# Latent projections of a fused transformer kernel: loads in order of use and in pieces, the first two weight units side by side, one PSUM bank per output

## The chip, the cores and the metric

The kernel runs on one core of a Trainium2 chip. The metric is the device time of one execution in microseconds. The time before is the median of three executions.

## The reference, cut to what matters

The reference is a stack of three transformer blocks on 512 tokens of width 1024. The first one begins with latent attention. Its opening, which the change touches, is:

```python
h = rms_norm(x, attn_pre_g[0])
a = h @ w_a                                   # 1024 x (384 + 256 + 64)
cq, ckv, kr = jnp.split(a, [384, 640], axis=-1)
q  = rms_norm(cq, g_q) @ w_uq                 # 8 heads of 128 + 64
kv = rms_norm(ckv, g_kv) @ w_ukv              # 8 heads of 128 + 128
# rotary embedding of the 64-wide parts with cos, sin of positions; attention; w_o;
# y = x + rms_norm(attention @ w_o); FFN (silu(gate) * up) @ down; a second attention block
# with a relative bias, and its FFN; a third block: gated attention, a 31-tap convolution,
# and an FFN with a 3-tap convolution on gate and up; a last rms_norm
```

## The kernel before, in words

Activations lie transposed: 128 rows of the width on the partitions, 512 tokens along the free axis, so x is eight tiles of 128x512. All products are of fp32 accuracy made from three products of shorter floats: every operand is split into a high and a low part, and `product` issues high x high, low x high, high x low (lines 350 to 352).

The weights come as a stream of 307 units of 128x1024 (eight 128x128 blocks each), in the order in which TensorE uses them. Each unit passes four engines, through two buffers of each kind:

- SP loads it into `raw` (`load_units`, line 321); the load of unit u waits for the low part of unit u-2.
- ACT rounds it into `whi` in `round_unit` (line 326). Each call takes the next unit, `turn["act"]`, and waits for its load and for TensorE's last product of unit u-2. The calls stand at fixed places in ACT's program, between its other work.
- POOL subtracts and writes the low part `wlo` (`low_units`, line 336).
- TensorE waits for `wlo` in `next_unit` (line 342) and does the unit's 24 matmuls.

ACT's program before calls `round_unit` 8 times in `latents_act`, then 12 times in the MLA heads, 8 in its output projection, 66 in the first FFN, 24 in block B, 8 in its output projection, 66 in the second FFN, 28 in the first half of block C, 7 in its heads, 16 in the merge and 66 in the last FFN: 309 calls. Calls beyond unit 306 do nothing. TensorE uses 6, 12, 8, 66, 24, 8, 66, 28, 7, 16 and 66 units in the same stages.

Between the blocks stand the joins j0 to j3 (`join_pe`, `join_act`, `join_dve`): the residual is added tile by tile, each new tile of x is split and multiplied by one unit at once, its square is summed on TensorE (`pe_sum`, line 463), and at the end `act_root` and `dve_inverse` make the norm's factor. `join_act` has no call of `round_unit`. After j0 and j2 ACT's next work is `ffn_act`, whose first statement is a call; after j1 it is `b_first_act`, after j3 `c_first_act`, with a call first as well.

In the latents, TensorE (`latents_pe`, line 523) multiplies unit 0 by the tiles of x as these are split, with a sum of squares after each tile, then units 1 to 5 (cq, cq, ckv, ckv and the rotary key), with a sum for each earlier output in between. The outputs take banks 0, 1 and 2 in turn. DVE (`latents_dve`) makes the low parts of x and, between them, steps of the sine and cosine tables (`dve_table`). ACT (`latents_act`) issues five loads, rounds unit 0, splits and squares the tiles of x, and makes the sines.

In the last FFN (`ffn_act`, `ffn_dve` with `conv`) each step has a gate unit and an up unit. DVE scales a half (L458), ACT applies Identity with a gain (L984), DVE adds two taps (L1016, L1019), ACT applies Silu (L991), DVE multiplies (L1027) and splits (L1029, L1031). ACT's order in a step is: call, Identity of the gate, call, Identity of up, Silu.

Of the kernel before, what the change touches and what calls it, by code (L numbers as in the profile page):

```python
# [125 lines left out]
def column_map(items):  # L126
    at, where = 0, {}
    for name, n in items:
# [5 lines left out]
GAINS = [("pre0", 8), ("post0", 8), ("fpre0", 8), ("fpost0", 8), ("gq", 3), ("gkv", 2), ("kvsrc", 8),  # L134
# [4 lines left out]
CONSTS = [("ident", P), ("ones", P), ("cdist", 4 * 32), ("cmask", 4 * 32), ("cvalid", 4 * 32), ("inv", 1),  # L139
          ("sgn", 1), ("eps", 1), ("dist", T), ("maskA", T)]  # L140
# [68 lines left out]
def build(nc, x_in, pos_in, stream, gains_in, consts_in, rel_in, w1_in, out):  # L209
# [83 lines left out]
    def gg(name, k=0, n=1):  # L293
        return gn[:, GAIN_AT[name][0] + k:GAIN_AT[name][0] + k + n]

    ident, ones = cc("ident"), cc("ones")


    raw_in = [Signal(nc, f"raw_loaded{j}", 16) for j in range(2)]
    x_got = [Signal(nc, f"x_loaded{j}", 16) for j in range(2)]  # L300
    gains_got, consts_got = Signal(nc, "gains_loaded", 16), Signal(nc, "consts_loaded", 16)
# [12 lines left out]
    every = raw_in + x_got + bias_got + w1_got + [  # L314
        gains_got, consts_got, pos_got, mask_got, rel_got, rel_put, bias_put, out_put, w_hi, w_lo, proj, summed, scored,
# [174 lines left out]
    ang, kk_, rr = rope_tmp  # L490

    def dve_table(e, n):

        if n:
            e.wait_ge(*(made.at("sin") if n == 9 else made.at("cos") if n == 16 else formed.at(("table", n - 1))))
# [11 lines left out]
        elif n in (5, 12):  # L507
            op = e.scalar_tensor_tensor(rr[:, :], kk_[:, :], -c1, ang[:, :], ALU.mult, ALU.add)
        elif n in (6, 13):
            op = e.scalar_tensor_tensor(rr[:, :], kk_[:, :], -c2, rr[:, :], ALU.mult, ALU.add)  # L510
        elif n in (7, 14):
            op = e.scalar_tensor_tensor(rr[:, :], kk_[:, :], -c3, rr[:, :], ALU.mult, ALU.add)
        elif n == 8:
            op = e.tensor_scalar(rr[:, :], rr[:, :], PI32, -PI32, ALU.min, ALU.max)
        elif n == 15:
            e.tensor_scalar(rr[:, :], rr[:, :], float(np.pi / 2), None, ALU.add).then_inc(*formed.done("quarter"))
            e.wait_ge(*formed.at("quarter"))
            op = e.tensor_scalar(rr[:, :], rr[:, :], PI32, -PI32, ALU.min, ALU.max)
# [3 lines left out]

    def latents_pe(e):
        u = next_unit(e)
        for k in range(KD):
            e.wait_ge(*low.at(("pre0", k)))
            mm = product(e, u, k, bank[0][:, :], hh[:, k, :], hl[:, k, :], k == 0, k == KD - 1)
            if k == KD - 1:
                mm.then_inc(*proj.done(("a", 0), ("unit", u)))
            e.wait_ge(*squared.at(("x", k)))  # L530
            pe_sum(e, 7, tmp[k % 2][:, :], k == 0, k == KD - 1, ("x", k))
        for m in range(1, 5):
            if m >= 3:
                e.wait_ge(*evicted.at(("a", m - 3)))
            project(e, m % 3, hh, hl, ("a", m))
            e.wait_ge(*squared.at(("a", m - 1)))
            if m == 4:
                e.wait_ge(*stats.at((("x", 7), "mean")))
            pe_sum(e, 6 if m < 4 else 7, tmp[(m - 1) % 2][:, :], m in (1, 4), m == 3, ("a", m - 1))
        e.wait_ge(*evicted.at(("a", 3)))  # L540
        project(e, 0, hh, hl, "kr")
        e.wait_ge(*squared.at(("a", 4)))
        pe_sum(e, 7, tmp[0][:, :], False, True, ("a", 4))

    def latents_act(e):
        e.dma_start(gn[:, :], gains_in).then_inc(*gains_got.done(0))
        e.dma_start(cst[:, :], consts_in[:, 0:n_fixed]).then_inc(*consts_got.done(0))
# [1273 lines left out]
```

## Time and profile before

| | before |
|---|---|
| time, median of 3 runs | 2263.82 us (2262.23 to 2268.28) |
| profiled execution, its own time | 2264.33 us |
| its span | 2262.3 us |
| TensorE (PE) busy | 2137.6 us, 94% |
| DVE busy | 1031.2 us, 46% |
| ACT busy | 750.2 us, 33% |
| POOL busy | 750.2 us, 33% |
| DMA | 178.59 MB, mean 79 GB/s |

The span is what the trace covers; the time of that same execution is 2.0 us more. Busy times are sums over the whole span and hide which engine is waited for at which place. A row of a timeline gives start, duration, engine, line of the kernel, instruction, output and inputs, and in brackets how long the engine had been idle and whom it had waited for.

### The profile page before, as it was taken

How to read it: one execution, taken by the hardware profiler on the slowest of the kernel's cores; microseconds unless marked ns; L12 is line 12 of the kernel's file. 1: busy time of each engine (PE TensorE's matmuls, PEld its weight loads, DVE VectorE, ACT ScalarE, POOL GpSimd, SP SyncE). 2: the span in 40 equal slices, each digit the busy share in tenths (PEclk: the TensorE clock that was granted, in tenths of full speed). 3: DMA queues.
4: the chain of work that ended last, by engine and by line, in shares of the span. 5: the costliest groups of instructions: out<-in, count | busy, mean ns of one | idle time of the engine just before them, and what ended most of it. 6: DMA issues, size and time to landing. Idle time of an engine off the chain costs nothing.

```text
span 2262.3 us, 22596 instructions
## 1 busy us (share of the span) xinstructions
PE 2137.6 (94%) x8948; PEld 1620.6 (72%) x8948; DVE 1031.2 (46%) x1620; ACT 750.2 (33%) x1213; POOL 750.2 (33%) x311
## 2 busy tenths in 40 slices
PE   6898999999989999999999998898899999999998
PEld 4554778888856776668888885676655587888886
DVE  5543254442134333254444006994544356777511
ACT  4443332222234333332222223122554434333321
POOL 2211334444422222224444442432110143444442
PEclk9998999999999999999999999897799999999999
DMA  3410223232211222113232232221100122233232
GB/s 128 133 54 29 74 67 102 93 102 95 94 64 64 71 75 75 52 57 101 93 101 95 94 102 84 75 75 36 39 29 19 37 94 84 94 97 99 93 102 84
DMA packets 51815, 178.59 MB, mean 79 GB/s; under 512 B 5472, under 2 KB 5488, under 8 KB 51456
## 3 DMA queue, kind: packets, MB, share of 16 engines
q1 hardware_dynamic: 45264, 163.07, 22.2%
q10 hardware_dynamic: 6448, 14.09, 1.8%
q8 instruction: 71, 1.16, 0.2%
q14 instruction: 32, 0.26, 0.0%
HBM read 175.00 MB, written 6.33 MB: 80 GB/s over the span
## 4 chain that ended last, share of the span: by engine, by line
PE 81%; DVE 14%; ACT 3%; issue 1%; DMA 0%; POOL 0%; DVEq 0%; SPq 0%; ACTq 0%
PE bank L350 22%; PE bank L352 22%; PE bank L351 22%; PE bank L373 6%; DVE tmp L1352 4%; PE bank L438 4%; PE bank L424 2%; PE bank L464 1%; DVE hl L481 1%; DVE x L926 1%; DVE tmp L1656 1%; DVE tmp L924 1%; PE bank L832 1%; DVE rs L477 1%; ACT swapA L625 1%
## 5 line engine op out<-in xcount | busy, mean ns | idle before, releaser
L339 POOL TENSOR_TENSOR wlo<-raw,whi 128x1024 fp32r<-128x1024 f32 x307 | 750.0, 2443 | 1490.5 <-ACT whi L334 1490.4
L350 PE MATMUL bank<-hh,whi 128*128 128x512 f32 x1576 | 639.5, 406 | 58.2 <-DVE hl L481 29.4
L334 ACT ACTIVATE whi<-raw 128x1024 fp32r<-128x1024 f32 x307 | 324.9, 1059 | 1076.7 <-PE bank L352 1070.8
L351 PE MATMUL bank<-hl,whi 128*128 128x512 f32 x1576 | 622.7, 395 | 0.0
L352 PE MATMUL bank<-hh,wlo 128*128 128x512 f32 x1576 | 621.6, 394 | 0.0
L350 PEld LDWEIGHTS bank<-hh,whi 128*128 128x128 f32 x1576 | 301.6, 191 | 158.6 <-issue 50.5
L351 PEld LDWEIGHTS bank<-hl,whi 128*128 128x128 f32 x1576 | 302.1, 192 | 65.1 <-issue 5.1
L352 PEld LDWEIGHTS bank<-hh,wlo 128*128 128x128 f32 x1576 | 301.5, 191 | 64.7
L458 DVE TENSOR_TENSOR tmp<-bank,rs 128x512 f32<-128x512 f32 x159 | 109.3, 689 | 229.4 <-PE bank L352 224.9
L350 PE MATMUL bank<-fh,whi 128*128 128x512 f32 x528 | 205.4, 389 | 0.0
L351 PE MATMUL bank<-fl,whi 128*128 128x512 f32 x528 | 205.4, 389 | 0.0
L352 PE MATMUL bank<-fh,wlo 128*128 128x512 f32 x528 | 205.4, 389 | 0.0
L1027 DVE TENSOR_TENSOR tmp<-tmp,tmp 128x512 f32<-128x512 f32 x66 | 121.4, 1839 | 48.6 <-ACT tmp L991 46.3
L351 PEld LDWEIGHTS bank<-fl,whi 128*128 128x128 f32 x528 | 99.1, 188 | 20.7
L352 PEld LDWEIGHTS bank<-fh,wlo 128*128 128x128 f32 x528 | 99.1, 188 | 20.5
L350 PEld LDWEIGHTS bank<-fh,whi 128*128 128x128 f32 x528 | 99.1, 188 | 20.4
L1352 DVE SCALAR_TENSOR_TENSOR tmp<-zpad,gn,tmp 128x512 f32<-128x512 f32 x116 | 110.6, 1023 | 0.0
L1039 DVE COPY y<-bank 128x512 f32<-128x512 f32 x16 | 11.0, 687 | 204.1 <-PE bank L352 204.1
L1016 DVE SCALAR_TENSOR_TENSOR tmp<-tmp,gn,tmp 128x511 f32<-128x511 f32 x44 | 80.5, 1828 | 45.1 <-ACT tmp L984 45.1
L432 ACT ACTIVATE PT<-bank 128x128 f32<-128x128 f32 (+3 forms) x160 | 66.8, 435 | 101.5 <-PE bank L424 99.8
L350 PE MATMUL bank<-oh,whi 128*128 128x512 f32 x192 | 75.7, 394 | 5.1 <-DVE ol L1596 2.2
L352 PE MATMUL bank<-oh,wlo 128*128 128x512 f32 x192 | 75.4, 393 | 0.0
(210 smaller groups left out, 2180.7 us busy)
## 6 DMA issues: line engine op xcount, KB each, us to landing
raw<-stream SPq DMA_DIRECT2D x307, 512.0 KB, 3.4
bias_scratch<-rel_scratch ACTq DMA_DIRECT2D x1, 4096.0 KB, 19.0
biasB<-bias_scratch ACTq DMA_DIRECT2D x16, 256.0 KB, 3.9
x<-x_in SPq DMA_DIRECT2D x2, 1024.0 KB, 9.8
w<-w_in ACTq DMA_DIRECT2D x2, 1024.0 KB, 5.9
out<-y ACTq DMA_DIRECT2D x8, 256.0 KB, 2.2
cst<-consts_in ACTq DMA_DIRECT2D x1, 577.5 KB, 7.1
gn<-gains_in ACTq DMA_DIRECT2D x1, 318.5 KB, 4.3
```

The costliest lines, as they stand in the source:

```text
L334: e.activation(whi[u % 2][:, :], raw[u % 2][:, :], ACT.Copy).then_inc(*w_hi.done(u))
L339: e.tensor_tensor(wlo[u % 2][:, :], raw[u % 2][:, :], whi[u % 2][:, :].bitcast(F32), ALU.subtract)\
L350: e.matmul(o, wh, h, start=first, stop=False)
L351: e.matmul(o, wh, l, start=False, stop=False)
L352: return e.matmul(o, wl, h, start=False, stop=last)
L373: mm = e.matmul(bank[b][:, SPOT[t][1]:SPOT[t][1] + W(t)], qf[:, t * P:(t + 1) * P], kf[:, 0:W(t)], start=i == 0, stop=i == len(pieces) - 1)
L432: e.activation(PT[:, 0:t + 1, t * P:(t + 1) * P], bank[b][:, 0:W(t)].rearrange("p (k c) -> p k c", c=P), ACT.Copy).then_inc(*spread.done(( ...
L438: mm = e.matmul(bank[7][r0:r1, k * P:T], vf(k), PT[:, k, k * P:T], start=first and k == 0, stop=last and k == QT - 1, skip_group_check=not ...
L458: e.tensor_tensor(dst, bank[bk][:, :], r[:, :], ALU.mult).then_inc(*evicted.done(key))
L1016: e.scalar_tensor_tensor(acc[:, 1:T], u[:, 0:T - 1], gg("fdw", (r * KF + j) * 3 + 1), acc[:, 1:T], ALU.mult, ALU.add).then_inc(*formed.don ...
L1027: e.tensor_tensor(u[:, :], u[:, :], g[:, :], ALU.mult).then_inc(*formed.done((key, "product", j)))
L1352: e.scalar_tensor_tensor(s, zp[:, tap:tap + T], gg("dw", c * TAPS + tap), s, ALU.mult, ALU.add)\
```

## The change

- `GAINS` and `CONSTS` are reordered, so that what the latents need comes first, and both are loaded in two pieces; ACT issues seven loads instead of five. SP issues unit 0 first, then x in four pieces of two tiles, with unit 1 behind the second piece.
- Unit 0 is rounded and its low part made in two halves (`w_hi` and `w_lo` get a key 0.5). The second half is rounded behind the first tile of x.
- `latents_pe` runs units 0 and 1 side by side: at step k tile k by unit 0, the sum of tile k-1, tile k-2 by unit 1. Each of the five outputs has a bank of its own (0 to 4), kr takes bank 0 again, the sums use banks 6 and 7. The last sum (of output 4) is moved into `mla_pe`, behind the first MLA unit. That unit no longer waits for the low part of output 4, the second one does.
- The cosine's argument gets a tile of its own, `quarter`. Sine and cosine are made one after the other, behind the root of x. DVE does two table steps after each of the eight tiles.
- The calls of `round_unit` in `latents_act` stand at other places.

```diff
     def low_units(e):
-        for u in range(n_units):
+        e.wait_ge(*w_hi.at(0.5))
+        e.tensor_tensor(wlo[0][:, 0:512], raw[0][:, 0:512], whi[0][:, 0:512].bitcast(F32), ALU.subtract).then_inc(*w_lo.done(0.5))
+        e.wait_ge(*w_hi.at(0))
+        e.tensor_tensor(wlo[0][:, 512:1024], raw[0][:, 512:1024], whi[0][:, 512:1024].bitcast(F32), ALU.subtract)\
+            .then_inc(*w_lo.done(0))
+        for u in range(1, n_units):
...
-    def next_unit(e):
+    def next_unit(e, part=0):
         u = turn["pe"]
         turn["pe"] += 1
-        e.wait_ge(*w_lo.at(u))
+        e.wait_ge(*w_lo.at(part or u))
         return u
...
     def latents_pe(e):
-        u = next_unit(e)
+        u, v = next_unit(e, 0.5), turn["pe"]
+        for k in range(KD + 2):
+            if k == KD // 2:
+                e.wait_ge(*w_lo.at(u))
+            if k == 2:
+                next_unit(e)
+            if k < KD:
+                e.wait_ge(*low.at(("pre0", k)))
+                mm = product(e, u, k, bank[0][:, :], hh[:, k, :], hl[:, k, :], k == 0, k == KD - 1)
+                if k == KD - 1:
+                    mm.then_inc(*proj.done(("a", 0), ("unit", u)))
+            if 1 <= k <= KD:
+                if k == 1:
+                    e.wait_ge(*consts_got[0].at(0))
+                e.wait_ge(*squared.at(("x", k - 1)))
+                pe_sum(e, 7, tmp[(k - 1) % 2][:, :], k == 1, k == KD, ("x", k - 1))
+            if k >= 2:
+                mm = product(e, v, k - 2, bank[1][:, :], hh[:, k - 2, :], hl[:, k - 2, :], k == 2, k == KD + 1)
+        mm.then_inc(*proj.done(("a", 1), ("unit", v)))
+        project(e, 2, hh, hl, ("a", 2))
+        project(e, 3, hh, hl, ("a", 3))
+        for m in range(2):
+            e.wait_ge(*squared.at(("a", m)))
+            pe_sum(e, 6, tmp[m % 2][:, :], m == 0, False, ("a", m))
+        project(e, 4, hh, hl, ("a", 4))
+        e.wait_ge(*squared.at(("a", 2)))
+        pe_sum(e, 6, tmp[0][:, :], False, True, ("a", 2))
+        e.wait_ge(*evicted.at(("a", 0)))
+        project(e, 0, hh, hl, "kr")
+        e.wait_ge(*squared.at(("a", 3)))
+        e.wait_ge(*stats.at((("x", 7), "mean")))
+        pe_sum(e, 7, tmp[1][:, :], True, False, ("a", 3))
...
     def latents_act(e):
-        round_unit(e)
-        e.wait_ge(*gains_got.at(0))
-        e.wait_ge(*consts_got.at(0))
+        e.wait_ge(*raw_in[0].at(0))
+        e.activation(whi[0][:, 0:512], raw[0][:, 0:512], ACT.Copy).then_inc(*w_hi.done(0.5))
+        e.wait_ge(*gains_got[0].at(0))
         for k in range(KD):
-            if k == 4:
-                round_unit(e)
-            if k % 4 == 0:
-                e.wait_ge(*x_got[k // 4].at(0))
+            if k % 2 == 0:
+                e.wait_ge(*x_got[k // 2].at(0))
             e.activation(hh[:, k, :], x[:, k, :], ACT.Copy, scale=gg("pre0", k)).then_inc(*high.done(("pre0", k)))
+            if k == 0:
+                e.activation(whi[0][:, 512:1024], raw[0][:, 512:1024], ACT.Copy).then_inc(*w_hi.done(0))
+                turn["act"] += 1
             if k >= 2:
                 e.wait_ge(*summed.at(("x", k - 2)))
             act_square(e, tmp[k % 2], x[:, k, :], ("x", k))
-            if k == 4:
-                e.wait_ge(*formed.at(("table", 8)))
-                e.activation(sinT[:, :], rr[:, :], ACT.Sin).then_inc(*made.done("sin"))
+            if k == 0:
+                round_unit(e)
         act_root(e, rs[0], ("x", 7))
         round_unit(e)
+        e.wait_ge(*formed.at(("table", 15)))
+        e.activation(sinT[:, :], rr[:, :], ACT.Sin).then_inc(*made.done("sin"))
+        e.activation(cosT[:, :], quarter[:, :], ACT.Sin).then_inc(*made.done("cos"))
+        round_unit(e)
         for m in range(5):
-            if m:
-                round_unit(e)
-            if m == 3:
-                act_root(e, rs[1], ("a", 2))
...
-            if m == 0:
-                e.wait_ge(*formed.at(("table", 15)))
-                e.activation(cosT[:, :], rr[:, :], ACT.Sin).then_inc(*made.done("cos"))
+            if m == 1:
+                round_unit(e)
+            if m == 2:
+                round_unit(e)
+            if m == 3:
+                act_root(e, rs[1], ("a", 2))
         e.wait_ge(*formed.at("rel_ends"))
         e.dma_start(rel_dram, rel[:, :]).then_inc(*rel_put.done(0))
         round_unit(e)
...
     def mla_pe(e):
         mla_unit_pe(e, 0, 0)
+        e.wait_ge(*squared.at(("a", 4)))
+        pe_sum(e, 7, tmp[0][:, :], False, True, ("a", 4))
         mla_unit_pe(e, 1, 0)
...
     def sync_program(e):
         x_v = x_in.rearrange("(k p) t -> p k t", p=P)
-        e.dma_start(x[:, 0:4, :], x_v[:, 0:4, :]).then_inc(*x_got[0].done(0))
         e.dma_start(raw[0][:, :], stream[0, :, :]).then_inc(*raw_in[0].done(0))
-        e.dma_start(x[:, 4:8, :], x_v[:, 4:8, :]).then_inc(*x_got[1].done(0))
-        e.dma_start(raw[1][:, :], stream[1, :, :]).then_inc(*raw_in[1].done(1))
+        for k in range(0, KD, 2):
+            e.dma_start(x[:, k:k + 2, :], x_v[:, k:k + 2, :]).then_inc(*x_got[k // 2].done(0))
+            if k == 2:
+                e.dma_start(raw[1][:, :], stream[1, :, :]).then_inc(*raw_in[1].done(1))
         load_units(e)
```

## Rows read from the trace of the kernel before

**Rows 1.** The page: span, and the group of the low parts (busy, mean ns).

```profile
span 2262.3 us, 22596 instructions
...
L339 POOL TENSOR_TENSOR wlo<-raw,whi 128x1024 fp32r<-128x1024 f32 x307 | 750.0, 2443 | 1490.5 <-ACT whi L334 1490.4
```

**Rows 2.** Timeline of the start, and the first MLA unit (start us, us).

```profile
3.62 1.28 ACT L334 ACT_TABLE_LOAD   x1 [3.62 <-issue]
10.58 1.06 ACT L334 ACTIVATE whi<-raw 128x1024 fp32r<-128x1024 f32 x1 [5.68 <-DMA raw<-stream]
11.72 2.36 POOL L339 TENSOR_TENSOR wlo<-raw,whi 128x1024 fp32r<-128x1024 f32 x1 [11.28 <-ACT whi L334]
...
14.77 0.76 PE L350 MATMUL bank<-hh,whi 128*128 128x512 f32 x1 [14.77 <-DVE hl L481]
...
69.94 0.80 PE L350 MATMUL bank<-cqh,whi 128*128 128x512 f32 x1
```

**Rows 3.** The chain that ended last, in the latents (start us, us).

```profile
16.39 1.71 PE bank L464 x2
...
46.70 0.86 PE bank L464 x2
47.56 0.23 PE bank L350
```

**Rows 4.** Timeline of the end of join j0, DVE, ACT and POOL.

```profile
296.20 0.69 DVE L469 TENSOR_SCALAR rs<-bank 128x512 f32<-128x512 f32 x1 [2.58 <-PE bank L464]
...
296.92 0.63 ACT L473 ACTIVATE rs<-rs 128x512 f32<-128x512 f32 x1 [3.57 <-DVE rs L469]
297.46 1.04 ACT L334 ACTIVATE whi<-raw 128x1024 fp32r<-128x1024 f32 x1
...
298.58 2.40 POOL L339 TENSOR_TENSOR wlo<-raw,whi 128x1024 fp32r<-128x1024 f32 x1 [26.79 <-ACT whi L334]
```

**Rows 5.** A gap of TensorE, and the stretch behind it (PE, PEld, DVE, ACT, POOL, PEclk, DMA).

```profile
61.40 1.92 PE L464 MATMUL bank<-tmp,cst 128*128 128x512 f32 x2 [2.01 <-ACT tmp L461]
...
61.40:65.00 3.60, 3.60 (x7) 2.17 (x8) 2.81 (x3) 2.09 (x3) 2.37 (x1) 0.53 0.00 0
```

**Rows 6.** Timeline of TensorE behind join j1.

```profile
694.30 0.77 PE L350 MATMUL bank<-h2h,whi 128*128 128x512 f32 x1 [4.28 <-DVE h2l L481]
```

**Rows 7.** Timeline of the merge, first tile.

```profile
1798.24 0.69 DVE L1653 TENSOR_TENSOR tmp<-bank,gsig 128x512 f32<-128x512 f32 x1 [7.50 <-PE bank L352]
...
1802.42 0.63 ACT L1636 ACTIVATE hh<-tmp 128x512 fp32r<-128x512 f32 x1 [3.06 <-DVE tmp L1656]
```

**Rows 8.** Timeline of one step of the last FFN, by engine.

```profile
2019.74 0.69 DVE L458 TENSOR_TENSOR tmp<-bank,rs 128x512 f32<-128x512 f32 x1 [0.36 <-PE bank L352]
2021.60 2.29 DVE L1016 SCALAR_TENSOR_TENSOR tmp<-tmp,gn,tmp 128x511 f32<-128x511 f32 x1 [1.17 <-ACT tmp L984]
2023.92 0.75 DVE L1019 SCALAR_TENSOR_TENSOR tmp<-tmp,gn,tmp 128x510 f32<-128x510 f32 x1
2024.78 0.69 DVE L1027 TENSOR_TENSOR tmp<-tmp,tmp 128x512 f32<-128x512 f32 x1
...
2020.77 0.80 ACT L984 ACTIVATE tmp<-tmp,gn 128x512 f32<-128x512 f32 x1
2021.47 0.62 ACT L991 ACTIVATE tmp<-tmp 128x512 f32<-128x512 f32 x1
...
2020.94 2.40 POOL L339 TENSOR_TENSOR wlo<-raw,whi 128x1024 fp32r<-128x1024 f32 x1 [2.90 <-ACT whi L334]
```

**Rows 9.** Timeline of TensorE and POOL in block C, two rows.

```profile
1430.99 0.76 PE L350 MATMUL bank<-hh,whi 128*128 128x512 f32 x1 [3.51 <-POOL wlo L339]
...
1454.91 7.14 POOL L339 TENSOR_TENSOR wlo<-raw,whi 128x1024 fp32r<-128x1024 f32 x1 [6.16 <-ACT whi L334]
```

**Rows 10.** Landing of the pieces of x; the chain's first transfer.

```profile
DMA to landing us min/median/max: 7.3/9.8/12.4
...
1.23 9.33 DMA raw<-stream
```

More of the change, by code:

```diff
@@ L296, in build @@
     ident, ones = cc("ident"), cc("ones")
+    N_FIRST, C_FIRST = GAIN_AT["kvsrc"][0], CONST_AT["cdist"][0]
     raw_in = [Signal(nc, f"raw_loaded{j}", 16) for j in range(2)]
-    x_got = [Signal(nc, f"x_loaded{j}", 16) for j in range(2)]
-    gains_got, consts_got = Signal(nc, "gains_loaded", 16), Signal(nc, "consts_loaded", 16)
+    x_got = [Signal(nc, f"x_loaded{j}", 16) for j in range(4)]
+    gains_got, consts_got = ([Signal(nc, f"{n}_loaded{j}", 16) for j in range(2)] for n in ("gains", "consts"))
     pos_got, mask_got = Signal(nc, "positions_loaded", 16), Signal(nc, "mask_loaded", 16)
@@ L490, in build @@
     ang, kk_, rr = rope_tmp
+    quarter = sb("rope_quarter", [P, T], Y + 4 * KB)
     def dve_table(e, n):
         if n:
-            e.wait_ge(*(made.at("sin") if n == 9 else made.at("cos") if n == 16 else formed.at(("table", n - 1))))
+            e.wait_ge(*(made.at("sin") if n == 16 else formed.at(("table", n - 1))))
         if n == 0:
@@ L507, in dve_table @@
         elif n in (5, 12):
[L508 to L512, printed above, removed]
+            op = e.scalar_tensor_tensor((rr, quarter)[n == 12][:, :], kk_[:, :], -c1, ang[:, :], ALU.mult, ALU.add)
+        elif n in (6, 7, 13, 14):
+            r = (rr, quarter)[n > 12][:, :]
+            op = e.scalar_tensor_tensor(r, kk_[:, :], -c2 if n in (6, 13) else -c3, r, ALU.mult, ALU.add)
         elif n == 8:
@@ L515, in dve_table @@
         elif n == 15:
-            e.tensor_scalar(rr[:, :], rr[:, :], float(np.pi / 2), None, ALU.add).then_inc(*formed.done("quarter"))
+            e.tensor_scalar(quarter[:, :], quarter[:, :], float(np.pi / 2), None, ALU.add).then_inc(*formed.done("quarter"))
             e.wait_ge(*formed.at("quarter"))
-            op = e.tensor_scalar(rr[:, :], rr[:, :], PI32, -PI32, ALU.min, ALU.max)
+            op = e.tensor_scalar(quarter[:, :], quarter[:, :], PI32, -PI32, ALU.min, ALU.max)
         elif n == 16:
@@ L523, in latents_pe @@
     def latents_pe(e):
-        u = next_unit(e)
-        for k in range(KD):
[L526 to L547, printed above, removed]
-        e.dma_start(pos_i[:, :], pos_in.to_broadcast([P, T])).then_inc(*pos_got.done(0))
-        e.dma_start(maskA[:, :], consts_in[:, n_fixed:n_fixed + T]).then_inc(*mask_got.done(0))
-        e.dma_start(rel[:, 255:575], rel_in).then_inc(*rel_got.done(0))
-        round_unit(e)
-        e.wait_ge(*gains_got.at(0))
-        e.wait_ge(*consts_got.at(0))
-        for k in range(KD):
-            if k == 4:
-                round_unit(e)
-            if k % 4 == 0:
-                e.wait_ge(*x_got[k // 4].at(0))
+        u, v = next_unit(e, 0.5), turn["pe"]
@@ L593, in latents_dve @@
             dve_low(e, hl[:, k, :], x[:, k, :], gg("pre0", k), hh[:, k, :], ("pre0", k))
-            if k < 7:
-                dve_table(e, next(tables))
-                dve_table(e, next(tables))
+            if k == 0:
+                e.wait_ge(*consts_got[0].at(0))
+            dve_table(e, next(tables))
+            dve_table(e, next(tables))
         dve_mean(e, rs[0], 7, D, ("x", 7))
-        dve_table(e, next(tables))
         dve_inverse(e, rs[0], ("x", 7))
@@ L637, in mla_unit_pe @@
             if (which, p) == (0, 0):
-                e.wait_ge(*low.at(("a", 4)))
+                e.wait_ge(*low.at(("a", 2)))
+                e.wait_ge(*evicted.at(("a", 4)))
             elif which == 0:
@@ L647, in mla_unit_pe @@
                 e.wait_ge(*evicted.at(("q1", p)))
+            if (which, p) == (1, 0):
+                e.wait_ge(*low.at(("a", 4)))
             c0, n = (0, 3) if which == 0 else (3, 2)
```

36 lines of the change are left out of this document (22 added, 14 removed).

## The prediction

> **What bounds the kernel now.** I read four views. First the page's span and costliest groups: 2262.3 us of span, and 307 low-part subtractions on POOL that hold POOL for only 750 us [rows 1]. The profiled run's own time is 2264.33 us, 2.0 us more than its span and within 0.03% of the median of the three runs, 2263.82 us, so a sum against the span carries over one to one. TensorE is 94% busy by the page, so nearly every microsecond in which it finds no rounded weights is lost. Second, the timeline of the start: the first matmul begins at 14.77 us, since the first weight unit is ready for ACT only at 10.58 us [rows 2]. This is what the change aims at. Third, the chain of work that ended last for prices of single matmuls [rows 3]. Fourth, the places after the latents where ACT's order decides when a weight unit is rounded [rows 4 to 9].
>
> The reader should keep one thing in mind: each weight unit goes raw, high part (ACT, `round_unit`), low part (POOL), TensorE. From the start of `round_unit` to the end of the low part it takes 298.58 + 2.40 - 297.46 = 3.5 us [rows 4]. A unit of 24 matmuls takes 24 x 0.227 = 5.44 us at the full clock. ACT must therefore start rounding a unit at least 3.5 us before TensorE asks for it.
>
> **The change, part 1: the lead of the rounding.** The diff shows no edit outside the latents and two lines of `mla_pe`, but it removes one call. Before, `latents_act` calls `round_unit` eight times (once ahead, k=4, after the root, four in m=1..4, once at the end). After, it rounds unit 0 by hand, then k=0, after the root, after the sines, m=1, m=2, end: seven units. All later calls stay where they are: 12 in the MLA, 8, 66, 24, 8, 66, 28, 7, 16, 66, together 301. So 309 calls for 307 units become 308. The call that stands at the place of unit n used to round n+2; now it rounds n+1, throughout the kernel. Where ACT has nothing to wait for between calls, this costs nothing: the call then waits for TensorE to leave unit n-1 anyway and starts 5.4 us before it is needed (the two plain FFN loops, their down projections, loop B, the MLA pairs: I followed ACT's order in each and find at least 0.5 us spare, except about 0.25 us at the two half-way points of the down projections, 0.5 us together). Elsewhere:
>
> *Joins (j0, j1, j2, j3).* `join_act` contains no rounding call. Before, the unit after the join is already rounded; after, its call comes behind `act_root`. In j0 that call starts at 297.46 and its low part ends at 300.98, while the last sum matmul ended near 296.1 [rows 4]. TensorE stands still 5.0 us. It also loses its clock: after a gap of 2.0 us the granted clock was 0.53 over 3.6 us, the lower of its two levels [rows 5], so half of about 3.2 us is lost, 1.5 us. j0, j2 and j3: 6.5 us each. j1: TensorE waits 4.3 us anyway for the second rounding of x, behind the POOL operation on the unit before [rows 6]; with kB one gap later I get its end 3.5 us late instead of 6.5. Together 23.0 us.
>
> *Merge.* The call for unit m+1 comes behind the copy of tile m-1. From the end of unit m-1: two scalings and an unblocked add (0.04 + 0.61 + 0.72 + 0.69), copy from +2.06, rounding at +2.6, ready at +6.2; before, the add was held until POOL was done and the copy came at +4.2 [rows 7]. Two units then take 6.2 + 5.44 = 11.64 instead of 10.88 us: 0.38 x 8 = 3.0 us, and 0.6 us for the first unit of the last FFN.
>
> *Last FFN (22 steps).* Let S be the start of DVE's scaling of the up half. After: Identity S+0.72, Silu S+1.42, rounding S+1.96, POOL S+3.10. DVE: two taps from S+1.56, 0.75 us each, product at S+3.20 [rows 8]. The product has two SBUF inputs and arrives 0.1 us after POOL has started; the row at 2021.60 shows what happens then: 2.29 instead of 0.75 us, done 0.55 us after POOL. So the product ends at S+6.1, the high and low parts at S+7.3, and only then is the next gate half scaled (7.35), activated (8.1) and its successor rounded (8.8), ready at 12.4 to 12.7 when it is wanted at 10.9 to 12.3. The steps alternate between about 12.3 and 11.3 us, mean 11.8 instead of 10.88: 22 x 0.9 = 19 us. If the product gets in first, the price is 22 x 0.15 = 3 us. I take the first, since the order follows from rows, though by 0.1 us only.
>
> *First half of block C.* The four convolutions are DVE's; TensorE already waits there (gaps of 3.5 us and one behind a POOL operation that took 7.14 instead of 2.40 us among back-to-back taps) [rows 9]. DVE hides most of a late unit. I find z and gate units up to 3 us late in single rounds and the second compressed projection 2.7 us late behind the last convolution: 5 us, bounds 1 (only part of the last term) and 12 (two more starved low parts, 4.7 us each). The Trainium skill, SBUF — State Buffer, "Who interferes with whom", says the loser of the shared ports waits for one whole instruction of the other; by that a low part would wait one tap, and the upper bound would be 6. The 7.14 us row differs from it.
>
> **Part 2: the start.** The first 1 MB that SP issues now is unit 0 and the first two tiles of x. Before, SP's first 1 MB landed 7.3 us after its issue, at 8.0, unit 0 (third half-MB) at 10.56, the last x at 14.2 [rows 2, 10]. So I put unit 0 at 5.3, x[0:2] at 8.0, unit 1 (fourth) at 12.4. The first pieces of the gains and constants are small and are asked for only with x at 8.0, so they cost nothing. ACT issues seven DMAs instead of five (some 0.55 us each), loads its table (1.28 us) and can round the first half at 5.8. TensorE's first product starts near 9.7, 5 us earlier. But the second call of `round_unit` (k=0) makes ACT wait for unit 1 at 12.4 before tile 1; its low part on POOL holds DVE's low part of tile 1 until 16.4. TensorE thus starts tile 1 at 16.5, at the lower clock until about 21. From there the loop is bound by TensorE: per k two products and a sum, 2 x 0.68 + 0.87 = 2.23 us [rows 3], ACT's and DVE's 2.1 us beside it. The pair ends near 35.8. Then the removed call bites for the first time: unit 2 is rounded only after the root, ready at 39.3, a gap of 3.5 us and again the low clock. Units 2, 3, two sums, 4, kr and two sums follow without a gap to 66.2. Unit 6, however, is now rounded by the last call, behind `rel_ends`, behind DVE's reciprocal and its last scaling: ready at 72.3. Before, it began at 69.94 [rows 2]. Price +2.4 us, bounds -4 (unit 1 lands with x[0:2], at 8) and +6 (x or unit 1 two microseconds later, one more clock drop). The bank for each output and the earlier sinT save nothing: no eviction was waited for longer than the sums there. Sine and cosine in one table, and the 17 table steps moved into the loop, lie under the 2.23 us.
>
> **Sum.** 2.4 + 23.0 + 3.6 + 19 + 5 + 0.5 = 53.5 us; 2264 + 53 = 2317 us.
>
> **Rivals.**
> A: the product on DVE wins its 0.1 us race in the last FFN. The sum falls by 16 to 2301 us. For it: 0.1 us is the error of such pitches. Against: all pitches are measured in one step that repeats every 10.88 us.
> B: contention in block C and at the start takes its upper bounds: 53.5 + 7 + 3.6 = 64, and 2328 us.
> C: the lead costs only at the joins and the start gains its 4: 23 + 1 - 4 + 4 (merge, halves) = 24, and 2288 us. It needs ACT to reach its calls about 1 us earlier than I find in the last FFN.
> D, on the other side: faster. The mechanism is the start: if unit 1 lands near 8, TensorE streams both units from there, the pair ends 7 us sooner and 5 us survive to 69.9, giving 2259 us; it decides only if the joins cost nothing, that is if the unit after a join is ready before its 8 sums end, thus if my count of calls is wrong. The count of the before kernel agrees with the trace (a rounding follows each root and its result is not asked for at once), so this is small.
> E: the change does not show, a gain at the start of about 20 us cancelling the joins: no row offers 20 us before 69.9 where TensorE's own work fills most of it.
>
> **Chances.** Forecast 0.45, A 0.25, B 0.13, C 0.10, D 0.04, E 0.03. Within 0.3%, about what a measurement of this kernel can tell from no change, is 2257 to 2271. Range 2290 to 2332: it holds the forecast, A and B, whose ends come from the bounds above, and leaves C, D, E. Faster 0.04, same 0.03, slower 0.93.
>
> **What would show it.** In the profile after: TensorE's first matmul near 9.7, the second tile's near 16.5; a gap near 36 and one before 72; in the waits, weight loads released by POOL's low part, some 5 us at each of three joins (before: none there); the last FFN's step at 11 to 12.3 us instead of 10.88, with the product at 2.9 us; the merge at 5.8 us a unit. The prediction is wrong if the unit after j0 starts within 1 us of the last sum, or if the last FFN keeps 10.88 us (rival A), or if the start ends over 5 us from 72.3.

## The result and the profile after

The changed kernel takes 2309.05 us (median of four runs, 2303.62 to 2316.00) against 2265.31 us for the kernel before in the same session: the ratio is 1.0195, 95% interval 1.0156 to 1.0234. It is slower, as forecast, and 8 us from the forecast of 2317. The four runs lie in two pairs: near 2303.7 us with a mean granted clock of 0.965 and 0.966, and at 2314.41 and 2316.00 us with 0.959 and 0.958. The profiled run is one of the shorter ones, 2303.70 us with a span of 2301.7 us; against the span before [rows 1] that is 39.4 us, and the account below is of these 39.4.

The page of the changed kernel, the span and the costliest groups (busy, mean ns | idle before, releaser):

```profile
span 2301.7 us, 22605 instructions
...
L345 POOL TENSOR_TENSOR wlo<-raw,whi 128x1024 fp32r<-128x1024 f32 x306 | 755.7, 2470 | 1515.3 <-ACT whi L335 1515.3
L356 PE MATMUL bank<-hh,whi 128*128 128x512 f32 x1576 | 647.1, 411 | 105.4 <-POOL wlo L345 72.6
```

The last row shows where to look: ahead of the first matmuls of this group TensorE stands 105.4 us in all (58.2 before), 72.6 of them for POOL's low part. (One low part of 307 stands outside the first group: unit 0 is now split in halves.)

The start, by the timelines of ACT, TensorE and POOL:

```profile
5.61 0.63 ACT L573 ACTIVATE whi<-raw 128x512 fp32r<-128x512 f32 x1
...
12.72 1.06 ACT L335 ACTIVATE whi<-raw 128x1024 fp32r<-128x1024 f32 x1 [4.83 <-DMA raw<-stream]
...
16.80 0.79 PE L356 MATMUL bank<-hh,whi 128*128 128x512 f32 x1 [6.90 <-DVE hl L487]
...
72.22 0.79 PE L356 MATMUL bank<-cqh,whi 128*128 128x512 f32 x1 [5.56 <-POOL wlo L345]
```

TensorE begins at 8.28 us instead of 14.77, then stands 6.90 us: ACT waits for unit 1, whose low part (13.85 to 16.20 on POOL) also holds up DVE's low part of the second tile. The first MLA unit starts at 72.22 against 69.94 [rows 2].

The end of join j0, where [rows 4] stood, and the stretches behind the four joins (columns behind the times: length, then PE, PEld, DVE, ACT, POOL, clock, share of the DMA engines, GB/s):

```profile
305.05 0.63 ACT L479 ACTIVATE rs<-rs 128x512 f32<-128x512 f32 x1 [3.59 <-DVE rs L475]
305.58 1.99 ACT L335 ACTIVATE whi<-raw 128x1024 fp32r<-128x1024 f32 x2
...
306.70 4.68 POOL L345 TENSOR_TENSOR wlo<-raw,whi 128x1024 fp32r<-128x1024 f32 x2 [28.40 <-ACT whi L335]
...
309.10 0.80 PE L356 MATMUL bank<-hh,whi 128*128 128x512 f32 x1 [4.81 <-POOL wlo L345]
```

```profile
309.10:312.60 3.50, 3.50 (x8) 2.81 (x9) 0.69 (x1) 0.63 (x1) 2.28 (x1) 0.50 0.67 163
695.20:698.70 3.50, 3.49 (x9) 2.80 (x10) 0.69 (x1) 3.03 (x5) 1.90 (x1) 0.58 0.68 211
1012.10:1015.60 3.50, 3.50 (x8) 2.78 (x9) 0.66 (x1) 0.63 (x1) 2.27 (x1) 0.50 0.59 163
1398.30:1401.80 3.50, 3.50 (x8) 2.76 (x9) 0.72 (x3) 0.00 (x0) 2.22 (x1) 0.50 0.96 398
```

Two units are rounded one behind the other, only after the root. The gap of 4.8 us stands behind each of the four joins. The granted clock in the 3.5 us behind it is 0.50 in three cases, the lower level (1.2 GHz), and 0.58 behind j1.

One step of the last FFN, where [rows 8] stood:

```profile
1965.66 0.47 PE L356 MATMUL bank<-hh,whi 128*128 128x512 f32 x1 [1.29 <-POOL wlo L345]
1977.05 0.47 PE L356 MATMUL bank<-hh,whi 128*128 128x512 f32 x1 [0.22 <-POOL wlo L345]
1989.48 0.47 PE L356 MATMUL bank<-hh,whi 128*128 128x512 f32 x1 [1.25 <-POOL wlo L345]
```

```profile
1967.49 2.40 POOL L345 TENSOR_TENSOR wlo<-raw,whi 128x1024 fp32r<-128x1024 f32 x1 [1.98 <-ACT whi L335]
```

```profile
1967.62 2.82 DVE L1056 TENSOR_TENSOR tmp<-tmp,tmp 128x512 f32<-128x512 f32 x1
```

The steps are 11.39 and 12.43 us long in turn, and DVE's product starts 0.13 us behind the low part and takes 2.82 us.

Two places that the prediction did not list. The first is in the MLA heads, after and then before:

```profile
152.18 3.42 DVE L415 TENSOR_SCALAR probsA<-probsA,stat 128x128 f32<-128x128 f32 x4
155.52 0.68 DVE L464 TENSOR_TENSOR tmp<-bank,rs 128x512 f32<-128x512 f32 x1
156.12 0.68 DVE L464 TENSOR_TENSOR kn<-bank,rs 128x512 f32<-128x512 f32 x1
```

```profile
143.17 1.28 DVE L409 TENSOR_SCALAR probsA<-probsA,stat 128x128 f32<-128x128 f32 x4
```

The low part that began at 152.96 us lies on the normalise instructions; the key's half behind them is late, and TensorE waits 2.8 us for `kn` instead of 1.74 at each further pair. In the kernel before, the same low part came at 146.20, behind these instructions. Over the whole stage (first MLA unit to first output unit, before and then after, columns as above) this is only a part of the loss:

```profile
69.94:224.39 154.45, 137.78 (x510) 84.07 (x508) 63.85 (x158) 68.83 (x147) 30.75 (x13) 0.93 0.22 72
72.22:235.10 162.88, 141.54 (x511) 86.67 (x511) 78.24 (x157) 66.87 (x144) 28.84 (x12) 0.91 0.21 68
```

Of the 8.4 us, TensorE stands 4.7 us longer, and for the rest it is busy longer (141.54 us against 137.78): the same matmuls take more time at a mean granted clock of 0.91 instead of 0.93.

The second is the end of the first FFN. In the kernel before, ACT's last rounding waits for the last down unit, and the squares of two tiles, copied for them at 645.73 and 647.09 us, wait behind it on ACT:

```profile
649.87 1.06 ACT L334 ACTIVATE whi<-raw 128x1024 fp32r<-128x1024 f32 x1 [4.38 <-PE bank L352]
650.83 1.13 ACT L461 ACTIVATE tmp<-y 128x512 f32<-128x512 f32 x2
```

```profile
651.48 2.42 DVE L839 TENSOR_TENSOR tmp<-tmp,tmp 128x512 f32<-128x512 f32 x1 [3.69 <-ACT tmp L461]
```

```profile
656.35 0.37 PE L852 MATMUL bank<-cst,tmp 128*128 128x1 f32 x1 [4.86 <-DVE tmp L839]
```

In the changed kernel the same sum of squares runs at 662.97 for 0.82 us, straight behind the copy that it needs, and TensorE has no gap there. This is a gain that the change brought by chance.

By stages, from TensorE's and ACT's rows at either end (span time before, after, and what the stage itself added):

| up to | before | after | stage | predicted |
|---|---|---|---|---|
| first MLA unit | 69.94 | 72.22 | +2.3 | +2.4 |
| first output unit | 224.39 | 235.10 | +8.4 | 0 |
| root of j0 | 296.92 | 305.05 | -2.6 | 0 |
| end of FFN 0 | 649.61 | 664.88 | +7.1 | +6.8 |
| root of j1 | 685.30 | 691.17 | -9.4 | 0 |
| second output stage | 930.58 | 938.02 | +1.6 | +3.5 |
| root of j2 | 1002.84 | 1008.02 | -2.3 | 0 |
| root of j3 | 1390.15 | 1394.20 | -1.1 | +6.8 |
| first half of block C | 1607.56 | 1623.78 | +12.2 | +11.5 |
| root behind the merge | 1891.02 | 1906.64 | -0.6 | +3.0 |
| end | 2262.3 | 2301.7 | +23.8 | +19.6 |

The measured column adds up to 39.4, the predicted one to 53.6 (its terms as they stood; the halves' 0.5 us are in the two FFN rows). Each measured number is from one execution of each kernel; how far such a number moves by itself is said below under what stays open.

### The profile page after: what moved, and what is told of

It reads as the page before. It is cut to its first block, busy times and chain, and to the rows that moved or that the text cites. A ratio compares the mean times of both kernels' runs of the same rounds, so it can differ in the third digit from the quotient of the medians.

```text
span 2301.7 us, 22605 instructions
## 1 busy us (share of the span) xinstructions
PE 2138.0 (93%) x8948; PEld 1615.7 (70%) x8948; DVE 1042.5 (45%) x1620; ACT 749.0 (33%) x1213; POOL 758.9 (33%) x312
## 4 chain that ended last, share of the span: by engine, by line
PE 76%; DVE 15%; POOL 3%; ACT 3%; issue 2%; DMA 0%; ACTq 0%; SPq 0%; DVEq 0%
PE bank L356 21%; PE bank L357 20%; PE bank L358 20%; PE bank L379 6%; DVE tmp L1381 4%; PE bank L444 4%; POOL wlo L345 3%; PE bank L430 2%; DVE tmp L1056 1%; PE bank L470 1%; ACT whi L335 1%; DVE hl L487 1%; DVE x L955 1%; DVE tmp L464 1%; DVE tmp L953 1%
## 5 line engine op out<-in xcount | busy, mean ns | idle before, releaser
L356 PE MATMUL bank<-hh,whi 128*128 128x512 f32 x1576 | 647.1, 411 | 105.4 <-POOL wlo L345 72.6
L1058 DVE TENSOR_SCALAR fh<-tmp 128x512 fp32r<-128x512 f32 x66 | 119.7, 1813 | 2.3
L1068 DVE COPY y<-bank 128x512 f32<-128x512 f32 x16 | 11.1, 692 | 213.6 <-PE bank L358 213.4
L1381 DVE SCALAR_TENSOR_TENSOR tmp<-zpad,gn,tmp 128x512 f32<-128x512 f32 x116 | 105.2, 976 | 0.0
L1056 DVE TENSOR_TENSOR tmp<-tmp,tmp 128x512 f32<-128x512 f32 x66 | 90.0, 1364 | 7.5 <-DVE tmp L1048 0.5
L1013 ACT ACTIVATE tmp<-tmp,gn 128x512 f32<-128x512 f32 x44 | 35.9, 816 | 171.6 <-DVE tmp L464 171.6
```

Of the source, the lines that this page charges most:

```text
L356: e.matmul(o, wh, h, start=first, stop=False)
L1056: e.tensor_tensor(u[:, :], u[:, :], g[:, :], ALU.mult).then_inc(*formed.done((key, "product", j)))
L1058: e.tensor_scalar(fh[:, j, :], u[:, :], 1.0, None, ALU.mult).then_inc(*formed.done((key, "high", j)))
L1381: e.scalar_tensor_tensor(s, zp[:, tap:tap + T], gg("dw", c * TAPS + tap), s, ALU.mult, ALU.add)\
```

## The experiments

Ratios are to the kernel before, measured beside each group of runs. Its medians were 2265.68 us (e1 to e4), 2265.42 us (e5 to e8) and 2260.37 us (e9 and e10, on another chip), so between groups the ratios are to be compared and not the times.

**One call back in the changed kernel.**

```
             if m == 3:
+                round_unit(e)
                 act_root(e, rs[1], ("a", 2))
```

> The changed kernel with one more round_unit(e) at m == 3 of latents_act, ahead of the root, so that every later call rounds unit n+2 again as before; all else of the change stays. If the lost lead is the cause of nearly all of the +43.8 us (my theory), this kernel is within 10 us of the kernel before: 2265.3 + the 2.3 us by which the changed kernel came later to the first MLA unit, less whatever the earlier rounding gives back, so 2260 to 2272; the four gaps of 4.8 us after the joins, the normalise instructions of 3.4 us, and the last FFN's steps of 11.4 and 12.4 us are gone. If instead the rest of the change (the new start, the bank for each output, the loads in pieces, the other places of gains and constants) brings the time, it stays at 2295 to 2315.

Measured: 2270.19 us, ratio 1.0014 [0.9999, 1.0029]. One line takes away 39 of the 43.7 us, the rest of the change untouched. Behind j0 TensorE has no gap, and the clock there is full (columns as above); the normalise instructions are a second row:

```profile
300.00:303.50 3.50, 3.50 (x17) 2.90 (x16) 2.34 (x3) 1.74 (x2) 1.62 (x2) 1.00 0.42 133
```

```profile
146.34 1.27 DVE L415 TENSOR_SCALAR probsA<-probsA,stat 128x128 f32<-128x128 f32 x4
```

The normalise instructions are back at 1.27 us, and the root of j0 falls at 296.94, that of j3 at 1390.2: as in the kernel before. So up to there the new start gains and loses nothing. It does have a gain at first: with the lead back, the first MLA unit starts at 64.99 us, 5.0 us ahead of the kernel before. But the next unit needs DVE's `qn`, which stands in DVE's program behind the rotary key; the key's last addition takes 2.71 us beside a low part (0.69 before), and `qn` begins at 75.56 us, against 75.38 before. TensorE waits out the whole gain:

```profile
76.39 0.77 PE L356 MATMUL bank<-cqh,whi 128*128 128x512 f32 x1 [6.21 <-DVE qn L464]
```

```profile
72.93 2.71 DVE L657 TENSOR_TENSOR krope<-tmp,swapA 128x512 f32<-128x512 f32 x1
```

**One call less in the kernel before.**

```
         e.dma_start(rel_dram, rel[:, :]).then_inc(*rel_put.done(0))
-        round_unit(e)
```

> The kernel before with its last round_unit(e) of latents_act taken out, and nothing else: later calls round n+1 instead of n+2. If the lost lead alone is the cause, this kernel shows the stages behind the first MLA unit as the changed kernel does (heads +8.4, four gaps of 4.8 us behind the joins, block C's first half +10, last FFN +23.8) and takes 2309 less the 2.3 us of the start: 2300 to 2312. If the cause is in the rest of the change, it stays near 2265.

Measured: 2307.33 us, ratio 1.0181 [1.0154, 1.0208]. The removed call alone, with nothing of the change, makes 42 of the 43.7 us, the whole loss within the scatter of the runs:

```profile
305.60 0.80 PE L350 MATMUL bank<-hh,whi 128*128 128x512 f32 x1 [4.82 <-POOL wlo L339]
```

Its last FFN (from the root behind the merge to the token root) takes 384.4 us, as in the changed kernel, against 360.6 before. These two runs together rule out the rival that the start, the pieces or the banks cost more than a few microseconds.

**The lead back for the last FFN alone.** One more `round_unit(e)` in `merge_act`, between the squares and the norm2 tiles.

> The changed kernel with one more round_unit(e) in merge_act, between the squares of x and the norm2 tiles, so that only the last FFN has the lead of before. If the length of the last FFN's steps comes from the lead, its steps go from a mean of 11.91 us back to 10.88 us and the kernel takes about 2309 - 24 = 2285 (2280 to 2291), with all earlier stages as in the changed kernel. If the steps' length comes from something else that the change left behind, it stays at 2305 to 2312.

Measured: 2283.17 us, ratio 1.0081 [1.0064, 1.0099]: 26 us less than the changed kernel. The product takes 0.69 us again (for example at 1970.94), the next at 1981.83, 10.89 us on; all gaps behind the joins are as in the changed kernel.

**The product ahead of the low part.** Two activations of one column hold ACT up before the first rounding of a step.

```
         for j in range(KF):
+            if conv and j:
+                for i in range(2):
+                    if (j, i) > (1, 0):
+                        e.wait_ge(*made.at((key, "pause", *((j, 0) if i else (j - 1, 1)))))
+                    e.activation(stat[:, 28:29], cc("eps"), ACT.Copy).then_inc(*made.done((key, "pause", j, i)))
             round_unit(e)
```

> The changed kernel with two activations of one column each ahead of the first rounding of every step of the last FFN but the first: ScalarE is held up by a few tenths of a us, and with it GpSimd's low part, which in the changed kernel starts 0.13 us ahead of VectorE's product. If the long steps come from VectorE's product meeting a GpSimd instruction that has just begun (product 2.82 us), the product now starts first, takes under 1.5 us, and most of the last FFN's +23.8 us goes: 2286 to 2296. If they come from the weights' low part being late for the matrix products whatever VectorE does, the delay adds to it or leaves it: 2305 to 2320. Nothing of the result is changed by the two activations.

Measured: 2312.56 us, ratio 1.0208 [1.0182, 1.0233]. My expectation fell. The product does go first, but POOL then begins in its middle, and the next instruction of DVE pays:

```profile
1989.61 0.69 DVE L1061 TENSOR_TENSOR tmp<-tmp,tmp 128x512 f32<-128x512 f32 x1
1990.34 2.51 DVE L1063 TENSOR_SCALAR fh<-tmp 128x512 fp32r<-128x512 f32 x1
```

```profile
1989.82 2.74 POOL L345 TENSOR_TENSOR wlo<-raw,whi 128x1024 fp32r<-128x1024 f32 x1 [3.04 <-ACT whi L335]
```

The groups of DVE in the last FFN (1950 to 2150 us) show it in three kernels. Before, the first taps pay, 1.33 and 2.29 us in turn; with the short lead the product; in this experiment the high part:

```profile
L1016 DVE SCALAR_TENSOR_TENSOR tmp<-tmp,gn,tmp 128x511 f32<-128x511 f32 x34 | 61.6, 1811 | 34.9 <-ACT tmp L984 34.9
L1027 DVE TENSOR_TENSOR tmp<-tmp,tmp 128x512 f32<-128x512 f32 x17 | 11.8, 693 | 1.8
```

```profile
L1056 DVE TENSOR_TENSOR tmp<-tmp,tmp 128x512 f32<-128x512 f32 x17 | 47.6, 2798 | 2.1 <-DVE tmp L1048 0.5
L1045 DVE SCALAR_TENSOR_TENSOR tmp<-tmp,gn,tmp 128x511 f32<-128x511 f32 x34 | 25.5, 751 | 30.1 <-ACT tmp L1013 30.1
```

```profile
L1063 DVE TENSOR_SCALAR fh<-tmp 128x512 fp32r<-128x512 f32 x17 | 40.5, 2384 | 0.6
```

In each kernel DVE loses about 2 us of a step to POOL (0.58 + 1.54 before; 2.80 against 0.69; 2.38 against 0.43). Before, TensorE does not wait for it: a rounded unit lies ready. What the short lead takes away is this cover. The two activations take 0.42 us of ACT and so make the low part a little later too, but a step now takes 12.06 us (TensorE at 1986.92 and 1998.98) where rival A priced some 11.0. Which of the two instructions goes first is not what decides; rival A of the prediction was wrong in kind, not only in its tenth of a microsecond.

**The short lead for the MLA alone.**

```
         mla_act(e)
+        round_unit(e)
         out_act(e, "oA")
```

> The changed kernel with one more round_unit(e) between mla_act and the first output stage, so that only the MLA heads run with the shorter lead. If the heads' +8.4 us come from the shorter lead (the low part then lands on VectorE's normalise instructions, 3.4 us in place of 1.27), they stay and all that follows is as in e1: 2270 + 8 = 2278 (2274 to 2283). If the heads' time came from the new start (other places of rows and buffers), e1 would have kept it; if instead the heads give nothing, this kernel equals e1 at 2270.

Measured: 2281.38 us, ratio 1.0069 [1.0049, 1.0089]. The group of the MLA's normalise instructions keeps 719 ns where e1 has 383, and TensorE still waits 2.78 us for `kn` at 123.70, 159.18 and 195.78 us; the root of j0 is at 303.26, 6.3 us behind that of e1, and so is that of j3 (1396.53 against 1390.25). Block C's first half is 4.9 us longer still than in e1, about which more below.

```profile
L415 DVE TENSOR_SCALAR probsA<-probsA,stat 128x128 f32<-128x128 f32 (+3 forms) x32 | 21.0, 719 | 0.3
```

**The second unit later in the start** (on top of e1). ACT rounds unit 1 behind the third tile of x, and TensorE asks for it only behind that tile's products with unit 0 (the lines below are ACT's part of the edit).

```
-            if k == 0:
+            if k == 2:
                 round_unit(e)
```

> The kernel e1_lead_back with the second unit's rounding behind the third tile of x on ScalarE (k == 2 in place of k == 0), and TensorE's wait for it behind the third tile's products with the first unit. In the changed kernel ScalarE stands 4.83 us waiting for the second unit, and TensorE has the second tile's products only at 16.80 us after a gap of 6.90 us. If that wait bounds the start, tiles 1 and 2 now run in the gap and the root of x comes two tiles' products at the low clock sooner, 2 x 3 x 0.43 = 2.6 us: 33 us in place of 35.4, and the whole takes 2270 - 2.6 = 2267.5 (2263 to 2271). Rival: ScalarE and VectorE pace the start tile by tile (or the first MLA unit waits on the roots and low parts), then the root moves by under 1 us and the total stays at 2266 to 2272.

Measured: 2267.37 us, ratio 1.0007 [0.9997, 1.0017]. The second tile starts at 11.20 us and the root at 32.46 instead of 35.38:

```profile
11.20 0.80 PE L356 MATMUL bank<-hh,whi 128*128 128x512 f32 x1 [1.08 <-DVE hl L487]
...
18.65 0.50 PE L356 MATMUL bank<-hh,whi 128*128 128x512 f32 x1 [1.32 <-POOL wlo L345]
```

The first output unit starts at 222.46, 3.6 us ahead of e1's 226.08 and 1.9 ahead of the kernel before. Of the 6.3 us by which the changed start began earlier, 1.9 are left there in this execution, and 3.6 at the roots of j0 to j3 (293.29 against 296.92, 1386.55 against 1390.15), once both faults (lead, unit 1) are mended. Neither shows in the time of the whole kernel, and both are less than what the same instructions vary by (see what stays open).

**The last calls behind the roots** (on top of e5, and then on the kernel before). This asks whether the 9.4 us at the end of the FFN can be kept without the short lead.

```
 def out_act:   for m in range(KD):
-            round_unit(e)
+            if m < KD - 1:
+                round_unit(e)
 ...
         token_root_act(e, key, y[:, KD - 1, :])
+        round_unit(e)
 def ffn_act:       for kk in range(KF // 2):
-                round_unit(e)
+                if conv or (half, kk) != (1, KF // 2 - 1):
+                    round_unit(e)
 ...
         token_root_act(e, (key, "down"), (x if conv else y)[:, KD - 1, :])
+        if not conv:
+            round_unit(e)
```

> e5_second_unit_later with the last rounding call of out_act and of ffn_act (for the two FFNs without taps) moved behind the token root, lead of two kept. In the kernel before, GpSimd's low part of that call blocks VectorE's sum of squares at each FFN's end (a gap of 4.86 us at 656.35), which the changed kernel does not have: from the end of FFN 0 to the root of join j1 it takes 26.3 us against 35.7 [before], and its output stages are 2.6 and 2.3 us shorter. If these savings come from where that one low part lands, this kernel has them with no gap behind the joins: 9 + 9 + 2.5 + 2.3 = 23 us, less up to 2.4 us at each of four places where the low part now meets VectorE's first joining tile: 2243 to 2256. If they come from the lead itself, nothing is won: 2262 to 2272.

> The kernel before with only the move of e6_calls_behind_roots (the last rounding call of each output stage and of the first two FFNs behind the token root). Same theories: 2265 - 23 = 2242, up to 2252 with the meetings in the joins, if where that low part lands is what costs; 2262 to 2268 if it is not. Against e6 it tells what the change's own start is worth once the lead is kept: within 3 us of each other by my reading of e1.

Measured: e6 2246.82 us, ratio 0.9917 [0.9894, 0.9940]; e7 2241.40 us, ratio 0.9889 [0.9866, 0.9912]. Both beat both kernels. In e7, at the end of FFN 0, the rounding comes behind the root and its low part begins where DVE stands idle between making the diagonal matrix of the norm's factors (L875) and the first joining tile; nothing of the join is held:

```profile
645.26 0.82 DVE L839 TENSOR_TENSOR tmp<-tmp,tmp 128x512 f32<-128x512 f32 x1
...
651.27 0.69 DVE L875 TENSOR_TENSOR tmp<-cst,stat 128x512 f32<-128x512 f32 x1
653.45 0.69 DVE L926 TENSOR_TENSOR tmp<-y,bank 128x512 f32<-128x512 f32 x1 [1.49 <-PE bank L861]
```

```profile
652.05 2.35 POOL L339 TENSOR_TENSOR wlo<-raw,whi 128x1024 fp32r<-128x1024 f32 x1 [6.52 <-ACT whi L334]
```

The first joining tile (two inputs, one in PSUM) took 0.69 us in the middle of the low part, so the up to 2.4 us that I had set aside for each meeting did not arise. Root to root, e7 gains 2.4 us to j0, 9.4 to j1, 3.1 to j2 and 8.3 to j3, 23.2 in all (1366.91 against 1390.15), where 23 were expected. (Of the 2.4, 1.7 us come and go without this move, as the next part shows.)

**Block C's calls ahead of the gates** (on top of e6, and of e7).

```
+            round_unit(e)
             for j in range(3):
-                round_unit(e)
+                if j < 2:
+                    round_unit(e)
                 gate_act(e, 3 * c + j)
```

> e6_calls_behind_roots with two rounding calls of each channel of block C taken ahead of the gate's activation for which they waited (unit n+2's rounding no longer stands behind VectorE's ten taps). In e6 the second and third of these channels each show one GpSimd group of 9.92 us for two low parts and then TensorE idle for 8.24 and 8.14 us; in block C's first half TensorE is idle 32.8 us. Theory 1 (two low parts asked for at once among back-to-back taps are what TensorE waits for): the groups of 9.92 us and the 8.1 us gaps go, and the kernel wins 8 to 16 us: 2231 to 2239. Theory 2 (VectorE's taps bound this half, it is busy 43.6 to 51 us of each 50 to 60): the gaps only change place, 2243 to 2249. Theory 3: the earlier low part meets more taps and VectorE loses by it, 2250 or more.

> The same move on e7_before_calls_behind_roots, that is on the kernel before with its old start. Theory 1: 2241 less 5 to 13 us (its TensorE idle time there is 28.2 us), 2228 to 2236. Theory 2: 2238 to 2244. Besides, e9 less e10 tells once more what the change's start brings when the lead is kept: by e5 (out stage begins 2 us earlier than in the kernel before) e9 should be 0 to 3 us shorter; e6 came out 5 us longer than e7, and if that is block C's play and not the start, it does not come back here.

Measured: e9 2243.45 us, ratio 0.9933 [0.9918, 0.9949]; e10 2242.42 us, ratio 0.9928 [0.9911, 0.9944]. The times lie in theory 2's ranges, but those were worked out on a kernel before of 2265 us, and here it took 2260.37. By the ratios the move won nothing and may have cost something: e9 has 0.9933 against e6's 0.9917, well within the intervals, and e10 0.9928 against e7's 0.9889, where the two intervals just touch. On a kernel before of 2265 us these ratios would make about 2250 and 2249 us, above the upper ends of theory 2 (2249 and 2244). Theory 1 was not put to the test: the groups of two low parts in a row were still there, since the move only changed which two units they were.

```profile
1442.10 9.93 POOL L345 TENSOR_TENSOR wlo<-raw,whi 128x1024 fp32r<-128x1024 f32 x2 [10.07 <-ACT whi L335]
```

e9 and e10, measured side by side, differ by 1.0 us: with the lead kept, the change's start is worth nothing that shows here, and the 5 us between e6 and e7 did not come back.

## Why the prediction was right, and where it was not

**The cause** was named before the run and is shown by two runs from both sides: e1 (one call added to the changed kernel: 2270) and e2 (one call taken from the kernel before: 2307). Rivals D and E are out by the time itself. Rival C is out as well, since giving the lead back in the last FFN alone (e3) takes away 26 us.

**Start**: +2.3 against +2.4, with both terms as forecast (second tile 16.80 against 16.5, first MLA unit 72.22 against 72.3). Only the first matmul came 1.4 us sooner than I had put it (8.28, not 9.7), which bought nothing.

**Joins**: a gap of 4.8 and the low clock behind it: +7.1 us over FFN 0 against 6.8 forecast. At j1 TensorE's one wait of 4.28 us [rows 6] became three, of 4.81, 1.53 and 1.74 us (695.21, 704.09 and 706.76); the stretch cost 1.6 us where 3.5 were forecast.

**Last FFN**: 23.8 against 19.6 us. The mechanism is right. The prediction rounded 22 x 0.9 = 19.8 down to 19; the mean step is 11.91 us, not 11.8, over 22 steps 2.4 us more; the rest of the difference, about 1 us, lies at the ends of the stage.

**Block C**: 12.2 against 11.5 (j3 with it). That this comes so near is luck: e3 and e4 carry out the same instructions up to there, and their stretch was 2.3 and 6.2 us longer than the changed kernel's, as said below.

**Merge**: this term was mis-sized: 3.0 forecast, and the merge took 0.5 us less than before (99.66 us from its first unit to the root, against 100.13). TensorE waits 0.69 to 0.75 us at every second unit as foreseen, but the wait before the sum at its end shrank: 2.18 us at 1900.75, against 4.18 at 1885.14 before.

**The step that failed** is the sentence that the calls elsewhere cost nothing, since "the call then waits for TensorE to leave unit n-1 anyway". I had followed only when a unit is ready for TensorE. I had not followed what a call holds up on its two engines. First, the low part lands at another moment on DVE: +8.4 us in the MLA heads, of which 3.8 are the lower clock behind more gaps. e8, with the short lead in the heads alone, starts the first output unit 6.3 us behind e1 (232.40 against 226.08), the changed kernel 9.0 us (235.10); of the 2.7 us between these two, 2.2 stand at the first MLA unit already (70.05 and 72.22), up to which their instructions are the same. Second, a call with the short lead no longer waits for the unit that is being multiplied, so what is queued behind it on ACT runs earlier: -9.4 us at each FFN's end, -2.6 and -2.3 us in the output stages. (Of the -2.6, 1.7 us aren't the call's: from the first output unit to the root of j0 e1 and e8 too, with the old lead there, take 70.86 us where the kernel before took 72.53 and the changed one 69.95.) At the root of j3 the same gain stands against the join's gap: -1.1 us measured, +6.8 forecast. The misses have both signs and leave 14 us on the profiled runs, so the total was nearer than its parts. That the median came within 8 us of 2317 is luck in part: it lies between two runs near 2303.7 and two near 2315.

**What stays open.** Block C's first half does not repeat, even with the same instructions. From the root of j3 to the table load ahead of the first root after the convolutions it takes, with the long lead, 194.9 us in the kernel before, 198.7 in e1, 204.4 in e5, 201.5 in e6, 199.8 in e7, 203.6 in e8 and 201.6 in both e9 and e10, though only e9 and e10 touch it; with the short lead 207.4 in the changed kernel, 210.9 in e2, 209.7 in e3 and 213.6 in e4. The changed kernel, e3 and e4 do the same work up to there. They differ in how many low parts took 7.1 instead of some 2.5 us among back-to-back taps: one, four and four (two in the kernel before).

```profile
1542.09 7.14 POOL L345 TENSOR_TENSOR wlo<-raw,whi 128x1024 fp32r<-128x1024 f32 x1 [6.16 <-ACT whi L335]
```

This is a row of e3. What sets their number is not shown, nor how much of the length they make; up to 6 us of a distance between any two of these kernels may be of this kind. The clock does the same in the MLA heads: e7 and e10 have the same instructions there (on two chips) and take 154.56 and 149.98 us, at a mean granted clock of 0.93 and 0.97.

## What to carry to other kernels

When a diff moves the start of a pipeline whose calls are spread over all the rest, count the calls: one less shifts every later one, and the price is paid wherever there was no slack. Then ask of each call two things, not one: when its result is ready for the consumer, and what stands behind it, on its own engine and on the one that does the next part. A call that waits for a unit still being multiplied belongs behind the short work that could run meanwhile; moving four of them won 1.1% on the kernel before, where the change itself, mended, won nothing that could be measured (e5: 1.0007).

## What the hardware showed unasked

A POOL operation among back-to-back taps of DVE can wait for more than one of them. In e6 two low parts begin at 1439.10 us amid ten taps, which run at their usual pitch, and take 9.92 us together, where two alone take 4.68; the sum behind the taps is then held itself:

```profile
1437.33 6.71 DVE L1387 SCALAR_TENSOR_TENSOR tmp<-zpad,gn,tmp 128x512 f32<-128x512 f32 x10
1444.07 2.71 DVE L1391 TENSOR_TENSOR zc<-tmp,tmp 128x512 f32<-128x512 f32 x1
```

```profile
1439.10 9.92 POOL L345 TENSOR_TENSOR wlo<-raw,whi 128x1024 fp32r<-128x1024 f32 x2 [6.82 <-ACT whi L335]
```

Here POOL got in only where the chain of taps broke: 1444.07 + 2.40 + 2.40 = 1448.9, and the group ends at 1449.02. That is no rule. Of the 15 low parts of e6 that begin amid taps in this half of block C, 13 got in at once and it was a tap that waited, as nine microseconds earlier, where ten taps take 8.80 us instead of 6.71:

```profile
1429.79 2.50 POOL L345 TENSOR_TENSOR wlo<-raw,whi 128x1024 fp32r<-128x1024 f32 x1 [6.16 <-ACT whi L335]
```

```profile
1428.02 8.80 DVE L1387 SCALAR_TENSOR_TENSOR tmp<-zpad,gn,tmp 128x512 f32<-128x512 f32 x10
```

No run shows what decides between the two.

The Trainium skill, SBUF — State Buffer, "Who interferes with whom", says that whoever of the two issues first keeps the shared ports for its whole instruction and the other blocks. The held instructions above (0.43 to 2.51, 0.69 to 2.82, 0.75 to 2.29 us) agree with it; the low part that waits about 5 us over some seven taps of 0.67 us does not follow from it.

Against a running low part, a product with one input in PSUM took 0.69 us (e7 at 653.45), one with both in SBUF 2.82 us (the changed kernel at 1967.62), and the rounding to the high part, SBUF to SBUF, 2.51 us (e4 at 1990.34) where it takes 0.43 alone.

A gap of TensorE does not always cost the clock. The changed kernel, e1, e3 and e4 have the same instructions up to the first matmul of unit 2 (39.41, 39.43, 39.86 and 38.88 us), and each has a gap of 3.42 to 3.44 us before it; over the 3.5 us behind that gap the granted clock was 0.64, 1.00, 0.50 and 0.70. Behind the gap of 4.8 us after j0 it was 0.50 in the changed kernel, e2, e3 and e4 alike.

```profile
39.43:42.93 3.50, 3.50 (x15) 2.92 (x16) 2.61 (x2) 2.07 (x3) 2.40 (x1) 1.00 0.47 154
```

The row is e1's.
